# A Mamba-2 / sparse-attention / PEER step on one Trainium2 core: expert rows gathered inside the opening of the sample's state stage

## The reference, cut to what matters

```python
xdt = xc * dtc[..., None]
decay_to_end = jnp.exp(a_cum[:, :, -1:] - a_cum)
chunk_states = jnp.einsum('bclgn,bclgjp->bcgjpn', Bc, xdt * decay_to_end[..., None])
h_last = h * d_c[..., None, None] + s_c
```

```python
act = jax.nn.gelu(jnp.einsum('nd,nhkd->nhk', h, peer_u[experts]))
return jnp.einsum('nhk,nhkd->nd', (g * act), peer_v[experts])
```

## Time and profile before

| | |
|---|---|
| median of 3 runs | 2726.63 us (2724.88 to 2726.69) |
| the profiled execution | 2727.99 us |
| its span, first to last instruction | 2726.0 us |
| busy: PE, VectorE, ScalarE, GpSimd | 2013.4, 1463.7, 663.9, 1472.5 us |
| gathers of expert rows | 62.3% of the 16 DMA engines' span |
| moved in all | 843.32 MB, mean 309 GB/s |

### The profile page before, as it was taken

One profiled execution on the slowest core, in us unless ns is written; L12 is line 12 of the kernel. 1 busy time (PEld: TensorE's weight loads), 2 busy tenths in 40 slices (PEclk: granted clock), 3 DMA queues, 4 the chain that ended last, 5 costly groups with the idle time before them and its releaser, 6 DMA issues. The chain is left out here.

```text
span 2726.0 us, 31394 instructions
## 1 busy us (share of the span) xinstructions
PE 2013.4 (74%) x10926; PEld 1272.5 (47%) x10926; DVE 1463.7 (54%) x3522; ACT 663.9 (24%) x1977; POOL 1472.5 (54%) x1487
## 2 busy tenths in 40 slices
PE   8999989988877989989989935754177776554054
PEld 6778865666655657644454622332154442111010
DVE  4421023247999965557621769778776764016800
ACT  5441026224545210025611122310021110000000
POOL 1110000016566865647644777777767777557775
PEclk9999989989987999989989967767589997877577
DMA  5424454446886999979889889999999999999998
GB/s 182 169 78 140 141 182 158 163 151 226 293 325 201 400 377 369 374 285 371 317 348 397 291 286 391 412 392 326 382 353 411 411 410 394 403 386 409 352 406 311
DMA packets 209781, 843.32 MB, mean 309 GB/s; under 512 B 25753, under 2 KB 32729, under 8 KB 190105
## 3 DMA queue, kind: packets, MB, share of 16 engines
q0 software_dynamic: 170912, 644.95, 62.3%
q1 hardware_dynamic: 38712, 196.36, 19.3%
HBM read 821.80 MB, written 23.54 MB: 310 GB/s over the span
## 5 line engine op out<-in xcount | busy, mean ns | idle before, releaser
L3658 POOL DMA_INDIRECT e_ring<-in_peer_u,e_idx x523 | 613.2, 1173 | 301.9 <-DVE e_dot L3822 139.0
L3822 DVE CUSTOM_DVE_ANT_0 e_ring<-e_ring,e_h 128x1024 f32<-128x1024 f32 x523 | 632.7, 1245 | 73.0 <-DMA e_ring<-in_peer_u,e_idx 25.8
L3658 POOL DMA_INDIRECT e_ring<-in_peer_v,e_idxT x487 | 506.0, 1039 | 261.6 <-issue 133.7
L3725 PE MATMUL ps<-e_ring,e_wz 128*32 128x512 f32 x1948 | 323.2, 712 | 269.4 <-DMA e_ring<-in_peer_v,e_idxT 147.4
L3725 PEld LDWEIGHTS ps<-e_ring,e_wz 128*32 128x32 f32 x1948 | 67.3, 121 | 427.3 <-issue 423.4
L371 PE MATMUL ps<-hT_ahead,wb 128*128 128x320 f32 x384 | 114.4, 454 | 0.0
L371 PEld LDWEIGHTS ps<-hT_ahead,wb 128*128 128x128 f32 x384 | 75.4, 201 | 31.2 <-issue 6.0
L3866 DVE TENSOR_TENSOR e_x<-e_x,ps 128x512 f32<-128x512 f32 x10 | 6.4, 683 | 145.7 <-PE ps L3725 145.7
L3725 PE MATMUL ps<-ring_pair,e_wz 128*32 128x512 f32 x152 | 69.7, 797 | 17.9 <-DMA e_ring<-in_peer_v,e_idxT 11.3
L1861 POOL CAST ra_atf<-ra_at 128x32 f32<-128x32 uint32 x8 | 1.7, 212 | 149.7 <-DVE ra_hit L1854 149.7
L1229 POOL MEMSET inda<- 128x256 f32 x1 | 0.3, 312 | 147.7 <-POOLq L4133 147.7
(11 more groups left out here) (789 smaller groups left out, 4577.3 us busy)
## 6 DMA issues: line engine op xcount, KB each, us to landing
wb<-in_weights SPq DMA_DIRECT2D x65, 1024.0 KB, 7.8
e_ring<-in_weights SPq DMA_DIRECT2D x36, 1024.0 KB, 4.9
wb<-in_late_weights SPq DMA_DIRECT2D x6, 2048.0 KB, 11.1
room<-in_late_weights SPq DMA_DIRECT2D x6, 2048.0 KB, 16.3
h<-in_weights SPq DMA_DIRECT2D x10, 1024.0 KB, 8.7
xs<-in_weights SPq DMA_DIRECT2D x9, 1024.0 KB, 7.9
e_ring<-in_peer_u,e_idx POOLq DMA_INDIRECT x523, 9.2
e_ring<-in_peer_v,e_idxT POOLq DMA_INDIRECT x487, 9.8
```

What stands on the lines that cost most here:

```text
L3658: nc.gpsimd.indirect_dma_start(out=self.room(place), out_offset=None, in_=k.peer_u if kind == "u" else k.peer_v, in_offset=off).then_inc(s ...
L3725: last = nc.tensor.matmul(k.ps[32 * b:32 * b + 32, self.SUMS + i, :], self.wz[:, at:at + 32], self.room(self.v_at[n])[:, 512 * i:512 * i + ...
L3822: v.tensor_tensor_reduce(uu, uu, self.h[:, tile % 2, :], 1.0, 0.0, ALU.mult, ALU.add, self.dot[:, tile % 2, t:t + 1]).then_inc(self.dotted, 1)
```

## The change

- In the convolution stage the product of decay and step is made for the sample's rows too: for the second group two instructions (128 partitions, then 64) stand where one stood.
- In the query stage GpSimd runs its last hook, number 18, behind the naming of the last head instead of ahead of it.
- In the state stage GpSimd forms `xde` with one product, x by the combined factor, and the other product and its semaphore are gone.
- The state stage has 35 hooks instead of 32 for the same 112 places. GpSimd runs hook 0 behind the clearing of `cmask`, hook 1 behind the product and hook 2 behind the 8 copies. TensorE, ScalarE and VectorE run hooks 0 to 2 ahead of their loops; the 32 halves then have hooks 3 to 34.

```diff
--- before.py
+++ after.py
@@ -624,8 +624,9 @@
 
             def split_sums():
                 dve.wait_ge(sums_read, 1)
-                c = slice(t0, t0 + NTP)
-                own(v.tensor_tensor(k.to_end[:, c, :], k.to_end[:, c, :], k.dt[:, c, :], ALU.mult))
+                for lo, hi, r in spans:
+                    c = slice(t0 + lo, t0 + hi)
+                    own(v.tensor_tensor(k.to_end[0:r, c, :], k.to_end[0:r, c, :], k.dt[0:r, c, :], ALU.mult))
                 dve.wait_ge(sums_turned, 1)
                 n = PARTS * HEADS
                 own(v.tensor_copy(k.acT[0:n, :], k.ps[0:n, 5, 0:NP]))
@@ -1983,11 +1984,13 @@
             for i in range(HOOKS):
                 if i == 10:
                     ex.ahead = ex.u_at[P * t0] + (TOPK if t0 else 8)
-                ex.pool(i)
+                if i < HOOKS - 1:
+                    ex.pool(i)
                 if i >= 4 and i % 2 == 0:
                     h = (i - 4) // 2
                     pool.wait_ge(marked, h + 1)
                     name_marked(nc.gpsimd, own, k, h, at[:, h % 2], hit[:, h % 2], atf, pick).then_inc(named, 1)
+            ex.pool(HOOKS - 1)
             if g.first:
                 pool.wait_ge(projected, HC)
                 ex.ahead = ex.NR
@@ -2149,12 +2152,13 @@
         h0_in = [sem(f"h0_in{i}") for i in range(NH0)]
         h0_out = k.h0_out
         x_in = sem("x_in")
-        (xdt_done, xde_done, cleared, masked, selected, turned, copied, decayed, read_out, contributed, updated,
+        (xde_done, cleared, masked, selected, turned, copied, decayed, read_out, contributed, updated,
          y_copied) = (
-            sem(n) for n in ("xdt_done", "xde_done", "cleared", "masked", "selected", "turned", "copied", "decayed",
+            sem(n) for n in ("xde_done", "cleared", "masked", "selected", "turned", "copied", "decayed",
                              "read_out", "contributed", "updated", "y_copied"))
         ex = k.ex
-        ex.plan(HALVES, k.share["state"])
+        EARLY = 3
+        ex.plan(EARLY + HALVES, k.share["state"])
         block = ctx.enter_context(nc.Block(no_gpsimd_drain=True))
 
         def seqs(i):
@@ -2181,14 +2185,15 @@
             x3 = k.xs[0:NS].rearrange("p (h q) -> p h q", q=HP)
             o3 = xde[:].rearrange("p (h q) -> p h q", q=HP)
             gp.memset(cmask[:], 0.0).then_inc(cleared, 1)
+            ex.pool(0)
             pool.wait_ge(x_in, 16)
-            gp.tensor_tensor(o3, x3, by_head(k.dt[0:NS, S, :], NS, HEADS), ALU.mult).then_inc(xdt_done, 1)
-            pool.wait_ge(xdt_done, 1)
-            gp.tensor_tensor(o3, o3, by_head(k.to_end[0:NS, S, :], NS, HEADS), ALU.mult).then_inc(xde_done, 1)
+            gp.tensor_tensor(o3, x3, by_head(k.to_end[0:NS, S, :], NS, HEADS), ALU.mult).then_inc(xde_done, 1)
+            ex.pool(1)
             pool.wait_ge(cleared, 1)
             for b in range(NB):
                 own = slice(DS * b, DS * b + DS)
                 gp.tensor_copy(cmask[:, :, b, own], k.CTs[:, :, own]).then_inc(masked, 1)
+            ex.pool(2)
             for q in range(HALVES):
                 j = q // 8
                 if q % 8 == 0:
@@ -2198,7 +2203,7 @@
                     mine = k.same[:, 0:NS:DS].rearrange("p (b a) -> p b a", a=1)
                     gp.tensor_tensor(bsel[:, j % 2], one.broadcast_to([NS, NB, STATE]),
                                      mine.broadcast_to([NS, NB, STATE]), ALU.mult).then_inc(selected, 1)
-                ex.pool(q)
+                ex.pool(EARLY + q)
 
         @block.tensor
         def _(pe):
@@ -2235,9 +2240,11 @@
                               start=(i == 0 and b == 0), stop=(i == 1 and b == HB - 1))
                 last.then_inc(read_out, 1)
 
+            for i in range(EARLY):
+                ex.pe(i)
             for q in range(HALVES + 1):
                 if q < HALVES:
-                    ex.pe(q)
+                    ex.pe(EARLY + q)
                     turn(q)
                 if q:
                     use(q - 1)
@@ -2248,9 +2255,11 @@
                 act.wait_ge(read_out, 8 * j + 8)
                 nc.scalar.copy(k.yn[:, 512 * j:512 * j + 512], k.ps[0:NS, 5, :]).then_inc(y_copied, 1)
 
+            for i in range(EARLY):
+                ex.act(i)
             for q in range(HALVES):
                 f, i = q // 2, q % 2
-                ex.act(q)
+                ex.act(EARLY + q)
                 act.wait_ge(turned, q + 1)
                 if q >= 2:
                     act.wait_ge(read_out, q - 1)
@@ -2266,11 +2275,12 @@
 
         @block.vector
         def _(dve):
-            ex.dve(0)
+            for i in range(EARLY + 1):
+                ex.dve(i)
             for q in range(HALVES):
                 f, i = q // 2, q % 2
                 if q + 1 < HALVES:
-                    ex.dve(q + 1)
+                    ex.dve(EARLY + q + 1)
                 dve.wait_ge(contributed, q + 1)
                 dve.wait_ge(decayed, q + 1)
                 hh = h0[f % NH0][:, seqs(i), :].rearrange("p b n -> p (b n)")
```

## The result

Sixteen runs of each kernel: 2703.3 us with the change (median, 2697.42 to 2715.79) against 2720.22 us before (2695.45 to 2737.46). The ratio is 0.9949, 95% interval 0.9929 to 0.997, so 8 to 19 us less, most likely 14. The three runs that stood ahead of the prediction, 2724.88 to 2726.69, were closer together than this kernel's runs are. The profiled execution has a span of 2695.9 us, 30 us less than the one before; where these 30 us lie is the first question.

A forecast was written before the change was run, and what follows sets the result against it. It took GpSimd's chain to set the time in the state stage's opening, and mostly DMA behind it. 0.7 - 0.4 + 3.5 - 0.1 + 0 = 3.7 us off 2726.63 gave 2722.9 us, range 2717.5 to 2728.5.

The forecast's parts named there:

- The naming order: End of the query stage: naming the last head first lets GpSimd's opening start at 1588.0, a gain of 0.7 us.
- x: State stage's opening: the load of x, queued beside gathers still in flight, loses 0.4 us (bounds 0 and 1.3).
- The product: State stage's opening on GpSimd: one product less gains 3.5 us, between 3.5 and 4.48.
- The product of steps: Convolution stage: one added VectorE instruction loses 0.1 us, between 0 and 0.22.
- The hooks: State stage's opening: seven earlier gathers, held by dots, delay the first contribution 9 us; net 0 (3.3 lost to 3.5 won).
- the rival "slower": State stage: halves keep 5.51 us each after a first contribution 9 us later, so 2735.6 us; chance 0.12.
- Full pace: Rival, state stage's opening: dots don't hold up the hooks' gathers, the DMA hole closes, 7.1 us won, 2719.5; chance 0.22.
- The inference of the Trainium skill: Gathers beside dots: two-input VectorE operations would not hold a gather up; the forecast went against it, citing 1.98 us.
- the own range: Whole kernel: 2720 to 2726 us around the main forecast, from the bounds of hooks and product; main forecast's chance 0.50.
- The base: Whole kernel: the median of 2726.63 us from which the forecast gain of 3.7 us was subtracted.

The follow-up runs named there:

- e13: Kernel before, with the 16 small gate loads of the cmp stage replaced by one load (rows get other gates): ratio 0.9975 to before.
- e14: Changed kernel, with the 16 small gate loads of the cmp stage replaced by one load (rows get other gates): ratio 0.9931 to before.
- e3: Kernel before, with only the last head's naming moved ahead of GpSimd's last query-stage hook: ratio 0.9995 to before.
- e7: Changed kernel, with ScalarE's end of the query stage also waiting for a small GpSimd memset behind its last gathers: ratio 1.0002 to before.
- e4: Kernel before, with only the product of steps and the single product of xde: ratio 1.0003 to before.
- e5: Kernel before, with only the three added hooks (two products, last head named behind the last hook): ratio 1.0005 to before.
- e6: Changed kernel without the three added hooks: ratio 0.9981 to before.
- e16: Changed kernel without the three added hooks, measured again: ratio 0.9969 to before.

## Why the prediction was wrong

The sign was right, the size was not: 3.7 us forecast, 14 measured (8 to 19), outside the range that I had given. The three measurements of the changed kernel, 0.9949, 0.9984 and 0.9965, weighted by their intervals, come to 0.9963, so 10 us, and the difference of e13 and e14 says 12. The traces place 5 to 9 us, by the reading: 7.6 by F2, 5.5 by D and 6.1 at the last contribution (means of four traces each), 7.8 and 8.7 by E. I take it as 8; that all of it is won by the end of the state stage stands on F2 alone. 8 us is inside the intervals of the second and third measurement and a hair outside the first. The 2 us to the mean of the three, and the rest up to 14, I can't attribute: two stretches that flip by some 8 and by up to 18 us in either kernel (the gates, and the gathers from the 1033rd on) are larger than what is left.

- **The naming order: this step failed.** "Then the naming takes 1572.6 to 1577.0 and the gathers 9.7 us plus 0.15 of issue, to 1586.8. ... The opening starts at 1586.8 + 1.2 = 1588.0, a gain of 0.7 us." I made the eight gathers one hook, which they are not, and I let the block's end wait for them. Nothing does: GpSimd passes it with gathers still to be issued. The right end is that of ScalarE's copies, 1581.4, 1.2 us ahead of the other engines' start, so SyncE's loads and VectorE's dots come 6.1 us earlier and only GpSimd's opening comes later, 1.6 us earlier than before. The next sentence fails with it, "What is late next is GpSimd's own sum of work, which is unchanged": since the dots run before x is there, the products and copies no longer take turns with them, and bsel ends 4.2 us earlier with this order alone (e3). Measured: 4.7 us instead of 0.7, and in the changed kernel 2.9 us go when the wait is put in (e7).
- **x.** It took 8.2 us from its issue to the product (1582.60 to 1590.80), not 5.35, behind gathers in flight: 2.9 us longer where I had taken 0.4 and bounded it at 1.3. It is there 3.3 us earlier all the same, since it was issued so much earlier.
- **The product.** 3.5 us less of GpSimd's opening, as forecast (e4), and a product alone takes 3.61 us (e3). By F2 the DMA engines keep 2.8 us of it, which is 3.5 within the scatter.
- **The product of steps** showed in none of the readings up to the 457th gather, but that gather comes anywhere from 1552 to 1560 us, so 0.1 us could not show. The added instruction itself takes 0.18 us.
- **The hooks.** Forecast 0, measured 0.3 to 0.4 us, which is 0. The mechanism was as described (gathers of 1.8 to 2 us beside dots), but milder: the dots first run out at 1602.4, since the first of them had started 6 us earlier, the copies took 2.26 us with one dot among them (1.24 alone), and the first contribution was 5.0 us late instead of 9. With two products and the late start (e5) it was 13.6 us late, and still nothing was lost at the end. So the rival "slower" has its premise and not its conclusion: halves of 3.2 rows go quicker, 158.0 us from the first to the last contribution against 170.9, so 5.10 us each, below the 5.22 that were to decide it.
- **Full pace** was given 0.22 and a price of 7.1 us, which is near the 8 us that the traces show, for the wrong reason: the DMA hole closed because the loads of x and the states and the dots moved, not because the hooks' gathers ran undisturbed. It is closed without hooks too (e6, e16).
- **The inference of the Trainium skill** ("SBUF — State Buffer", "Who interferes with whom") that a two-input VectorE operation doesn't hold up descriptor generation, made there for tensor_tensor, doesn't hold for the dots and the indirect DMAs of this kernel: 1.94 and 1.97 us for a gather beside dots in the changed kernel, 0.94 without. The gather at 1599.98, right at the start of a dot, was not held; the last section says which are.
- **Slips in the sum.** The hooks were worked out from x at 1593.4, which leaves out the 0.4 us lost on x; and the own range, 2720 to 2726, has the hooks win 2.7 us at most where the text above it has 3.5. Neither changes what failed.
- **The base.** The sum was laid on a median of three runs, 2726.63, of a kernel whose later medians were 2713 to 2720. A gain of 8 us would still have been inside the range against that base.

## What to carry to other kernels

Before an operation is moved to the end of a block, ask which engine's last instruction the others wait for: gathers that only stand in GpSimd's queue are free there, and every wait of another engine (here the last naming) belongs ahead of them. Where DMA is what fills the rest of the kernel, price a change of a serial opening by the time for which the DMA engines are fed earlier, by SyncE's loads too, not by when the first result comes: that was 13.6 us late in e5 and nothing was lost. And take each piece of the opening's work anew: what two engines did in turns goes quicker when one of them has done its share before. And when a kernel's executions differ by more than the gain, compare bytes moved from a common point and look for the one transfer that is sometimes late, before reading a single pair of traces.

## What the runs showed of the hardware that I had not expected

The end of a block that is built without a drain of GpSimd doesn't hold back the other engines for gathers in its queue: the first dot ran at 1582.76, 4.3 us ahead of the end of the last gather. A wait on a small instruction behind them holds them back (e7). Every block of this kernel is built so; none with a drain was tried.

Sixteen loads of 12-byte pieces can be late by 8 us. One or two issues of SyncE then take 3 to 11 us instead of 0.3, in 9 of 16 traces. One load of the same bytes in pieces of 96 bytes is issued in 0.34 us and was never late in four traces.

A gather is held by the dot that runs when it starts. In the twenty traces 4077 gathers started with over 0.6 us of a dot still to come. 3844 of them took 1.4 us or more; none ended less than 0.80 us behind the end of that dot, and 93 in 100 at most 0.83. The other 233 took 0.93 to 1.01 us; every one of these had started within 0.042 us of the dot's start, and that dot took 1.26 to 1.30 us instead of 1.22. Why these first 0.04 us matter was not tried.

Gathers and dots can fall into step. In the last stage of the kernel before a gather took 1.98 us and came once per two dots. In the changed kernel the same stretch went at one gather per dot, 1.28 us each:

```profile
2505.55 0.98 POOL L3668 DMA_INDIRECT e_ring<-in_peer_u,e_idx  x1 [0.30 <-issue]
...
2505.78 1.23 DVE L3832 CUSTOM_DVE_ANT_0 wb<-wb,e_h 128x1024 f32<-128x1024 f32 x1
2506.84 0.98 POOL L3668 DMA_INDIRECT e_ring<-in_peer_u,e_idx  x1 [0.30 <-issue]
```

There each dot starts 0.2 us behind a gather and, as I read it, rows land one at a time; in the earlier trace rows a stock of landed rows lets dots run without a pause, and the gather waits for each second one. Which of the two an execution takes is worth up to 18 us in this stretch (76.3 to 94.4 us over twenty traces). It is this alone which makes the difference: in all twenty traces the stretch is the sum of its 60 gathers and 18.3 us between them. In eight of them no gather takes over 1.3 us, and they are those of 76.3 to 76.5 us; in the others 1 to 23 gathers do. What puts an execution into one or the other was not tried.
